# A decoder layer's mixer rewritten on 64x64 diagonal blocks, tile by tile as a pipeline

## The reference, cut to what matters

```
gam = cumsum(g);  decay = exp(gam[:, None] - gam[None, :]) on and under the diagonal
A = strict_lower((k*beta) k^T * decay)
u, w = solve(I + A, [v*beta, k*beta*exp(gam)])     # unit lower triangular, per head and chunk
v_new = u - w S
o = (q*exp(gam)) S + causal(q k^T * decay) v_new
S = S * exp(gam_last) + (k*exp(gam_last - gam))^T v_new
```

## Time and profile before

| what | us |
|---|---|
| median of 3 runs | 1655.02 (1649.74 to 1659.88) |
| the profiled execution's own time | 1650.79 |
| its span, first to last instruction | 1649.0 |
| stages ahead of the mixer's first matmul | 367.49 |
| the mixer's 8 tiles, to the last MATMUL of L1436 | 367.49 to about 980.4 |
| the mixer's tail | 980.4 to 1013.54 |
| experts, embedding and final norm behind it | 635.46 |

### The profile page before, as it was taken

One profiled execution on the slowest core, in us unless ns is written; L12 is line 12 of the kernel. 1 busy time (PEld: TensorE's weight loads), 2 busy tenths in 40 slices (PEclk: granted clock), 3 DMA queues, 4 the chain that ended last, 5 costly groups with the idle time before them and its releaser, 6 DMA issues. The chain is left out here.

```text
span 1649.0 us, 19689 instructions
## 1 busy us (share of the span) xinstructions
PE 1466.5 (89%) x7404; PEld 1022.2 (62%) x7404; DVE 667.7 (40%) x1002; ACT 390.2 (24%) x730; POOL 286.1 (17%) x291
## 2 busy tenths in 40 slices
PE   6999999549989898988989985499999999939998
PEld 4579999435777768686968673345545455414443
DVE  2334551266546463647374633412112121124452
ACT  3213221114333333333333330011111111111211
POOL 0000000022232323132223220121222212100000
PEclk9999999759989998999899897699999999969999
DMA  5213232471020101111020104769999999633310
GB/s 187 77 39 102 81 97 66 64 234 51 7 74 13 68 25 54 38 41 61 19 80 0 45 3 142 243 240 346 343 342 350 347 352 337 270 126 109 109 70 26
DMA packets 149108, 217.57 MB, mean 132 GB/s; under 512 B 12491, under 2 KB 123675, under 8 KB 144446
## 3 DMA queue, kind: packets, MB, share of 16 engines
q1 hardware_dynamic: 130878, 169.15, 30.8%
q0 software_dynamic: 9504, 25.77, 4.1%
q10 hardware_dynamic: 8688, 22.14, 3.9%
HBM read 179.14 MB, written 42.54 MB: 134 GB/s over the span
## 5 line engine op out<-in xcount | busy, mean ns | idle before, releaser
L1690 PE MATMUL psum<-experts 128*128 128x512 f32 x528 | 234.4, 597 | 2.6 <-DVE experts L1712 2.6
L622 PE MATMUL psum<-split_parts 128*128 128x344 f32 x1224 | 194.1, 321 | 0.0
L622 PEld LDWEIGHTS psum<-split_parts 128*128 128x128 f32 x1224 | 193.9, 188 | 0.1
L1690 PEld LDWEIGHTS psum<-experts 128*128 128x128 f32 x528 | 100.9, 192 | 129.9 <-issue 126.7
L1039 POOL TENSOR_TENSOR decode_and_mix<-decode_and_mix,lasting 128x1024 f32<-128x1024 f32 x48 | 116.8, 2433 | 169.7 <-PE psum L1393 137.5
L1160 DVE TENSOR_TENSOR decode_and_mix<-decode_and_mix,psum 128x512 f32<-128x512 f32 x96 | 66.1, 688 | 173.0 <-PE psum L1407 173.0
L2065 PE MATMUL psum<-experts 128*128 128x512 f32 x288 | 127.3, 600 | 4.6 <-DVE experts L1976 4.6
L1727 DVE COPY experts<-psum 128x256 f32<-128x256 f32 x33 | 14.0, 425 | 274.9 <-PE psum L1697 274.9
L1706 PE MATMUL psum<-experts 128*128 128x512 f32 x264 | 119.2, 594 | 1.5 <-ACTq L1743 1.0
L1294 PE MATMUL psum<-decode_and_mix 128*128 128x512 f32 x256 | 114.5, 601 | 0.7 <-ACT decode_and_mix L1219 0.7
L1393 PE MATMUL psum<-decode_and_mix 128*128 128x128 f32 x768 | 103.6, 291 | 4.5 <-DVE lasting L1071 4.5
(11 more groups left out here) (357 smaller groups left out, 1889.4 us busy)
## 6 DMA issues: line engine op xcount, KB each, us to landing
experts<-in_w_gate SPq DMA_DIRECT2D x33, 1024.0 KB, 5.8
experts<-in_w_up SPq DMA_DIRECT2D x33, 1024.0 KB, 10.5
experts<-in_w_down SPq DMA_DIRECT2D x33, 1024.0 KB, 12.2
project<-in_w_in SPq DMA_DIRECT2D x18, 512.0 KB, 4.9
experts<-ye_d SPq DMA_DIRECT2D x16, 512.0 KB, 5.4
conv_out_d<-project ACTq DMA_DIRECT2D x12, 512.0 KB, 3.0
decode_and_mix<-conv_out_d SPq DMA_DIRECT2D x8, 768.0 KB
until_mixed<-in_x_prompt SPq DMA_DIRECT2D x8, 512.0 KB, 4.0
```

Source lines behind the costliest of these rows:

```text
L622: mm = nc.tensor.matmul(thirds(u)[:, b], w[:, u, k, :], x[:, k, b * TB:(b + 1) * TB], start=(i == 0 and k == 0), stop=(i == 2 and k == KD ...
L1690: mm = nc.tensor.matmul(bank(2 + s.v), xgT[s.v][:, k, :], wgu[s.u][:, k, :], start=(k == 0), stop=(k == KD - 1))
```

## The change

The mixer keeps its tiles of 128 tokens but treats each as two blocks of 64. The inverse is taken of the two 64x64 diagonal blocks of every head, which lie in the lower and the upper 64 partitions of one tile (`E_d`, `AT_d`, `QK_d`), so arrays that held 8x128 values in a row hold 8x64. The block below the diagonal (`AT_o`, `QK_o`, `E_o`) is kept apart and applied in the solve: first rows (`solve_first`), the carry into the second rows (`carry`), second rows (`solve_second`). LV becomes 6, with levels 1 to 5 in matmuls. Both the inverse and its transpose are carried on (`M_`, `MT`, side by side in `inv`), each by matmuls of its own, so that only level 0 is turned.

The matmuls of a level are 64x64 with 64 columns, and go by turns to the lower rows and columns of the array and the upper ones. The keys' products go to four 64x64 parts. The decay's sums and exponents are made for all tiles at once, where they don't need a matrix (`x8`, `kdec`, `egam`, `eglS`), and beta goes into the exponent by its logarithm. Attention reads q, k and v where they lie, without the four copies. The router's gain is folded into its weights once, and ACT instead of DVE moves the turned rows.

The order is a new one. Work of tile t+1 (rows, norms, decay, keys times keys) starts within tile t, the softmax is spread between the levels, and the projection is a single piece of 16 matmul calls behind the first solve. The h and xs rows are stored from SP's queue and not ACT's. All 8 tiles are written out instead of a loop. The diff, cut to its core; `lower` and `upper` are the two halves of the partitions, `bank(i)` is PSUM bank i:

```diff
-        def load_attention(sp, t, rows):
-            sp.dma_start(qst, qf[:, :, bass.ds(rows, P)]).then_inc(L("att_in"), 16)
-            sp.dma_start(kst, kf[:, bass.ds(rows, 2 * P)]).then_inc(L("att_in"), 16)
-            sp.dma_start(kswst, ksw[:, bass.ds(rows, 2 * P)]).then_inc(L("att_in"), 16)
-            sp.dma_start(vst.rearrange("p (a b) -> p a b", b=P), vt[:, bass.ds(t, 2), :]).then_inc(L("att_in"), 16)
...
+        def half_ps(g, part):
+            return bank(g)[:, part * 4 * HD:(part + 1) * 4 * HD].rearrange("p (s i) -> p s i", i=HD)
...
+                def offsets(t):
+                    g.wait_ge(S("x8"), 1)
+                    if t > 0:
+                        g.wait_ge(S("D"), t)
+                    g.tensor_tensor(X8M, bc(tile_of(x8, t), HD), bm(gaps, NH), ALU.add).then_inc(S("x8m"), 1)
...
+                for t in range(NT):
                     for l in range(1, LV):
...
-                            g.wait_ge(S("X1_ps"), (LV - 1) * t + l - 2)
                         elif l == 2:
                             g.wait_ge(S("MT1"), LV * t + 1)
-                        g.tensor_tensor(Lo[l % 2], AT, bm(cst[:, C_LV + l * P:C_LV + (l + 1) * P], NH), ALU.mult).then_inc(S("Lo"), 1)
-                tile(0, first=True)
-                with g.Fori(1, NT) as t:
-                    tile(t)
-                rms_pow("o", r8, m8, NH, NT - 1)
+                        else:
+                            g.wait_ge(S("X1_ps"), (LV - 1) * t + l - 2)
+                        g.tensor_tensor(Lo[l % 2], AT_d, bm(cst[:, C_LV + l * HD:C_LV + (l + 1) * HD], NH), ALU.mult).then_inc(S("Lo"), 1)
+                    if t < NT - 1:
+                        offsets(t + 1)
+                    R = rows_of(t)[0]
+                    rms_pow("x", rsx[0:R], msx[0:R], 1, t)
+                    if t < NT - 1:
...
+                def front_decay(t):
+                    v.wait_ge(S("gB_ps"), t + 1)
+                    v.wait_ge(S("x8m"), t + 1)
+                    V.tensor_tensor(E_d[lower], gB[lower, :, lower], X8M[lower], ALU.subtract)
+                    V.tensor_tensor(E_d[upper], gB[upper, :, upper], X8M[upper], ALU.subtract).then_inc(S("D_d"), 1)
+                    V.tensor_tensor(E_o[lower], gB[lower, :, upper], bc(tile_of(x8, t)[lower], HD), ALU.subtract).then_inc(S("D"), 1)
...
+                def front_system(t):
                     v.wait_ge(S("G_ps"), t + 1)
-                    v.wait_ge(S("Eb"), t + 1)
...
+                def level(t, l):
+                    for g in range(2):
+                        hs, cs = slice(4 * g, 4 * g + 4), slice(4 * g * HD, 4 * (g + 1) * HD)
+                        v.wait_ge(S(f"PT{g}_ps"), (LV - 1) * t + l)
+                        if l < LV - 1:
+                            V.tensor_tensor(inv[l % 2][:, :, cs], inv[(l - 1) % 2][:, :, cs], bank(g).rearrange("p (x n) -> p x n", x=2), ALU.subtract).then_inc(S(f"MT{g}"), 1)
+                        else:
+                            V.tensor_tensor(MT[l % 2][:, hs], MT[(l - 1) % 2][:, hs], half_ps(g, 1), ALU.subtract).then_inc(S(f"MT{g}"), 1)
...
+                for t in range(NT):
+                    front_system(t)
+                    if t > 0:
+                        logits(t - 1)
+                        gated(t - 1)
+                    queries(t)
+                    right_side(t)
+                    level(t, 1)
+                    from_state(t)
+                    biased(t, 0)
+                    level(t, 2)
+                    decay_state(t)
+                    maxima(t, 0)
+                    level(t, 3)
+                    biased(t, 1)
+                    maxima(t, 1)
+                    level(t, 4)
+                    normal(t, 0)
+                    gate(t)
+                    level(t, 5)
+                    normal(t, 1)
+                    first_rows(t)
+                    residual(t)
+                    second_side(t)
+                    second_rows(t)
+                    if t < NT - 1:
+                        front_norm(t + 1)
+                    updates(t)
+                    outputs_across(t)
+                    mean_square(t)
+                    normed(t)
+                    outputs(t)
+                    add_state(t)
+                    if t < NT - 1:
+                        front_scale(t + 1)
+                        front_decay(t + 1)
+                    output_norm(t)
+                logits(NT - 1)
                 gated(NT - 1)
...
+                def product(t, l):
+                    for g in range(2):
+                        act.wait_ge(S(f"X{g}_ps"), (LV - 1) * t + l)
+                        A.activation(Xs[:, 4 * g:4 * g + 4], half_ps(g, 0), ACT.Copy).then_inc(S(f"X{g}"), 1)
...
+                for t in range(NT):
+                    if t > 0:
+                        delta_rows(t)
+                    inverse_turned(t)
+                    product(t, 1)
+                    product(t, 2)
+                    product(t, 3)
+                    for i in range(GQA):
+                        exponential(t, 0, i)
+                    sink(t, 0)
+                    product(t, 4)
+                    for i in range(GQA):
+                        exponential(t, 1, i)
+                    sink(t, 1)
+                    product(t, 5)
+                    weights_turned(t, 0)
+                    row_squares(t)
+                    if t < NT - 1:
+                        squares(t + 1)
+                    weights_turned(t, 1)
+                    output_squares(t)
+                    if t < NT - 1:
...
+                def grams(i, f0):
+                    for f in range(4):
+                        for c in range(2):
+                            for a in (c, 1 - c):
+                                k = qkT[blocks[a], 4 + f, blocks[c]]
+                                if c == 0:
+                                    mm = T.matmul(psum[lower, i + a, :].rearrange("p (x s i) -> p x s i", x=2, s=4)[:, :, f], k,
+                                                  qkT[blocks[a], f0 + f, :].rearrange("p (x i) -> p x i", x=2), start=True, stop=True)
+                                else:
+                                    mm = T.matmul(psum[upper, i + a, f * HD:(f + 1) * HD], k, qkT[blocks[a], f0 + f, upper], start=True, stop=True)
+                    return mm
...
+                def product(t, l):
+                    for g in range(2):
+                        if l == 1:
+                            pe.wait_ge(S(f"M{g}"), t + 1)
+                        else:
+                            pe.wait_ge(S(f"MT{g}"), LV * t + l)
+                        pe.wait_ge(S("Lo"), (LV - 1) * t + l)
+                        for s in range(4 * g, 4 * g + 4):
+                            for b in blocks:
+                                mm = T.matmul(half_ps(g, 0)[b, s % 4, :], Lo[l % 2][b, s, :], M_[(l - 1) % 2][b, s, :], start=True, stop=True)
+                        mm.then_inc(S(f"X{g}_ps"), 1)
+                def correction(t, l):
+                    for g in range(2):
+                        pe.wait_ge(S(f"X{g}"), (LV - 1) * t + l)
+                        for s in range(4 * g, 4 * g + 4):
+                            for b in blocks:
+                                mm = T.matmul(half_ps(g, 1)[b, s % 4, :], Xs[b, s, :], MT[(l - 1) % 2][b, s, :], start=True, stop=True)
+                        if l < LV - 1:
+                            for s in range(4 * g, 4 * g + 4):
+                                for b in blocks:
+                                    mm = T.matmul(half_ps(g, 0)[b, s % 4, :], MT[(l - 1) % 2][b, s, :], Xs[b, s, :], start=True, stop=True)
+                        mm.then_inc(S(f"PT{g}_ps"), 1)
...
+                def solve_first(t):
+                    pe.wait_ge(S("r"), t + 1)
+                    pe.wait_ge(S("s0"), t + 1)
+                    for g in range(2):
+                        pe.wait_ge(S(f"MT{g}"), LV * t + LV)
+                        for s in range(4 * g, 4 * g + 4):
+                            mm = T.matmul(bank(4)[lower, s * HD:(s + 1) * HD], MT[1][lower, s, :], r_[lower, s, :], start=True, stop=True)
+                    mm.then_inc(S("p1_ps"), 1)
+                def carry(t):
+                    pe.wait_ge(S("u1"), t + 1)
+                    for s in range(NH):
+                        mm = T.matmul(bank(5)[upper, s * HD:(s + 1) * HD], AT_o[lower, s, :], u_[lower, s, :], start=True, stop=True)
+                    mm.then_inc(S("W_ps"), 1)
...
+                for t in range(NT):
+                    w = Projection(t)
+                    keys_queries(t)
+                    if t > 0:
+                        route(t - 1)
+                    state_rows_(t)
+                    if t > 0:
+                        turn_out(t)
+                    turn(t)
+                    scores(t, 0)
+                    for l in range(1, LV):
+                        product(t, l)
+                        correction(t, l)
```

(27 more changed lines are left out.)

787 lines of the change are left out of this document (410 added, 377 removed).

## The result

The changed kernel takes 1520.40 us, the median of 4 runs (1519.83 to 1534.47), against 1657.31 us for 4 runs of the kernel before. The ratio is 0.921, with a 95% interval of 0.915 to 0.927. The forecast was 1541, with 1500 to 1625 as its range.

A forecast was written before the change was run, and what follows sets the result against it. The prediction took TensorE's work to bound the mixer. Seven chain steps gave 60.4 us a tile, 62.5 with the clock; with start and tail, the gain was 112 us, so 1537 of span and 1541 predicted, range 1500 to 1625.

The forecast's parts named there:

- Step 1: Levels and first solve of a tile: a chain of matmuls, subtraction and hand-overs, with some softmax cost, 19.3 us.
- Step 2: The projection in one piece, 32 rows of 0.43 us, wholly on the tile's chain: 13.9 us.
- 3 to second rows: Turned weights, carry, next tile's rows, across, second solve, then DVE's copy: 6.0 us.
- Step 4: DVE's norms and mean square, then scaling of q and k waiting for POOL's two queued powers: 8.0 us.
- 5 to the start of `AT`: Columns, ACT's copy, keys times keys and latency, with the decays ending about level with it: 4.0 us.
- Step 6: DVE's `AT`, level 0, logits and gated output, with POOL's `Lo` delaying DVE twice by 1.0 us: 6.5 us.
- Step 7: DVE's queries, then the turn and first scores, partly behind them: 2.7 us.
- The clock's 2 us a tile: Addition to each tile for a lower granted clock where TensorE is sparse late in the tile: 2 us.
- Rival A: Quarters sharing a PSUM bank don't overlap: 58 ns a row, 72.5 us a tile, 1621 us in all; chance 0.14.
- Rival B: Half-filled array holds the clock down through the levels: 80.5 us a tile, 1685 us in all; chance 0.07.
- rival C: Slower or misordered hand-overs between engines, or late instructions: 68 to 74 us a tile, 1585 to 1633 us; chance 0.12.
- D: Better case, with no clock fall and hand-overs hidden: 57 us a tile, 1500 us in all; chance 0.07.

The follow-up runs named there:

- e5: e2 with the projection's matmuls of odd k, half of them, left out (output not the reference's): 1449.66 us.
- e3: The changed kernel with the levels' matmuls ordered as four heads of one array quarter, then four of the other, instead of by turns: 1543.31 us.
- e4: e2 with DVE's mean square of a tile issued ahead of the next tile's norm: 1505.79 us.
- e2: The changed kernel with POOL's `Lo` of levels 1 and 2 waiting for DVE's gated output of the tile before: 1507.10 us.
- e1: The changed kernel with three identity matmuls (six rows of 128 columns) added ahead of `turn_out`: 1518.44 us.
- e6: e2 with five of the projection's 16 matmul calls moved into the levels: 1500.53 us.
- e7: The changed kernel with the edits of e2, e4 and e6 together: 1499.60 us.

## Why the prediction was right, and where not

By its own steps, forecast and measured in the tile from 697.17, in microseconds:

| step | forecast | measured |
|---|---|---|
| 64x64 row | 0.032 | 0.029 |
| 1 levels, first solve | 19.3 | 19.56 |
| 2 projection | 13.9 | 13.84 |
| 3 to second rows (end of L1187) | 6.0 | 5.7 |
| 4 to the end of the scaling (L1092) | 8.0 | 7.8 |
| 5 to the start of `AT` (L1108) | 4.0 | 3.4 |
| 6 to the end of the gated output (L1219) | 6.5 | 6.1 |
| 7 and the clock | 2.7 + 2 | 5.0 |
| tile | 62.5 | 61.5 |

The reading of before was right: the mixer's time was TensorE's rows, and the change removes them (13.8 of the 15.3 us a tile). No run takes the smaller blocks and the new order apart, so what each would bring alone is open; e5 and e3 show that rows of the projection and of the levels go into the tile's length. Step 1 rested on the rate, which is the lower bound of the two given, and on the chain of hand-overs; in the trace a level takes 3.3 to 4.5 us. Step 2 is shown by e5. Step 4's cause, the two powers one behind the other, is shown by e4, though only half of what DVE won reached the tile. Step 6 named the right mechanism and counted it twice; e2 shows that the first hit was mostly hidden. In clean tiles the step takes 6.13 us with both hits (e1) and 4.89 without (e2), so they cost 1.24 and not 2.0, and 1.0 of the tile. Step 7 without the clock is 2.8 us in e1's clean tile, as forecast.

The clock's 2 us a tile had the right size for the profiled execution, 2.5, but not the right reason. I added them because TensorE would be as sparse in steps 6 and 7 as in the stretch from 778.6 of before, 1.01 us busy in 3.40. Ahead of the fall at 752.44 it was busy for 3.95 of 3.95 us, and for 4.08 of 4.75 before that. That the number came out so well is luck. The sums have two slips that change little: 60.4 and 2 are 62.4, and a second projection and 11 us are 24.9 and not 25.3.

Rival A, no overlap within a bank, has fallen. By the rule of the Trainium skill's page "TensorEngine Tiling (Array Packing)", section "Gotcha 1: PSUM Pressure", different row tiles cannot access one bank at the same time. The trace disagrees for this case: lower-left and upper-right quarters wrote one bank at 29 ns a row, where alone they start 58 ns apart in e3. Rival B, the clock held down through the levels, has fallen as well: levels run at 1.00, and the falls come behind them. Of rival C, neither the hand-overs nor the instructions' queue shows: q8 moved three times as many packets, and no idle time of the levels' matmuls is put down to issue. The 57 us a tile of D are what e4 (57.23) and e6 (57.17) reached in clean tiles, on top of e2, which took the hits on DVE away.

The stage: it began at 362.17 (363.6 forecast), the first product came at 386.66 (389), seven periods took 433.4 (437.5), and from the last first product to the end it was 77.8 (75); there the second projection began behind a wait for the last gated output and ran its first part at 1.2 GHz. The forecast for the profiled execution was 1539, and it took 1534.5. The rest of the distance, 14 us of the 21 between 1541 and 1520.4, is most likely the clock's term. I took the falls of the profiled trace, 2 us a tile, as something that every execution has, and added 2 us for the runs' median. In the changed kernel the profiled execution has a mean granted clock of 0.928 (and 0.930 in its second group), and of two more executions, which the median leaves out, one has 0.927 and took 1534.97 us; all others have 0.941 to 0.944, and take 14 to 17 us less in their groups. A mean of 0.928 over 1532.6 us is 221 us at 1.2 GHz, one of 0.942 over 1518 us 176; the 45 us between are about the seven falls of 6.8 us that the profiled mixer has. So I argue that the others lack most of these falls; it isn't shown, for only the profiled executions have a trace.

What decides whether a tile's clock falls is not settled. In the profiled execution of the changed kernel the fall came behind a stretch in which TensorE was busy nearly all the time, but with rows of few columns: L1646, 36 columns, and L1479, 64. e2 has the same rows, with TensorE as busy there (3.90 of 3.90 us from 735.10), and no falls from 451.85 to 799.66, six tiles; e7 has the same rows a little earlier and falls in five. The edits shift the tiles' period by a few tenths of a microsecond, and the falls come and go with it; whether the period is the cause no run shows.

## What to carry to other kernels

Rewriting a block triangular inverse on diagonal blocks that fill opposite quarters of TensorE pays by the rows that it removes, and the sum of rows times their measured rate along the chain, with each hand-over between engines, forecast the kernel's time within 2% (of the gain, 137 us, it foresaw 114). Before filling the waits of a dense chain of small matmuls, look at what a large one costs between them (1.1 us instead of 0.875 here): only waits longer than that are worth filling, and two calls brought as much as five. A GpSimd operation that need not run yet should wait for the VectorE instruction on the path that reads two SBUF operands; this one wait took 13.5 us off the median, more than every other edit. Of these, 1.0 us a tile is the hit on DVE itself, 8 in all, and the rest is not accounted for: by the traces the falls of the clock change with every edit.

## What the runs showed of the hardware

- Two 64x64 quarters that write different partitions of the same PSUM bank run side by side at 29 ns a row of 64 columns in float32. TensorE also pairs them over a change of quarter when they stand in separate groups of eight rows (36 ns on average).
- Two 512-column rows between 64x64 rows cost 1.1 us instead of 0.875 in a row of their own kind.
- A VectorE instruction with both inputs in SBUF that met a running GpSimd operation ended a little less than its own length behind that operation's end: 1.64 us instead of 0.69, 1.48 instead of 0.41. With the GpSimd operation moved away it had its own length again (e2).
- TensorE's granted clock fell to 1.2 GHz behind a stretch in which the engine was busy for 3.95 of 3.95 us. With six more rows of 128 columns (e1) two of seven tiles had a fall, of 3.4 us, instead of all seven with 6.8 or more.
- The same kernel's executions differed by 14 to 17 us together with their mean clock (0.927 to 0.930 against 0.941 to 0.944); the profiled one was among the long ones in both groups.
